# The last layer of the first block works on 258, then 256, of its 272 columns

## The chip, the cores and the metric

The kernel runs on one core of one Trainium2 chip. Its time is the device time of one execution in microseconds (us). Three executions of the kernel before took 2561.17, 2563.9 and 2571.58 us; the median is 2563.9 us.

## What is computed

The reference chains two blocks. The first block puts 16 meta tokens ahead of 256 text tokens, T = 272 in all, and runs two layers over them. The second block runs on the 256 text tokens alone. One layer of the first block, cut to what matters here:

```python
def first_block(...):
    h = jnp.concatenate([meta, x], axis=1)              # 16 + 256 tokens
    for l in range(DEPTH):                              # DEPTH = 2
        u = _rms_norm(h, norm_mix_pre[l])
        (a_q, ..., d_v, gate_logits) = jnp.split(u @ w_in[l], offsets, axis=-1)
        # four mixers: attention over all tokens, chunked recurrence in both directions, ...
        branches = jnp.stack([o_a, o_b, o_c, o_d], axis=2)
        gates = jax.nn.sigmoid(gate_logits.reshape(bsz, T, N_BRANCH, D_MODEL))
        merged = jnp.sum(jnp.einsum('btnw,nwd->btnd', branches, w_branch[l]) * gates, axis=2)
        h = h + _rms_norm(merged @ w_out[l], norm_mix_post[l])
        f = _conv_ffn(_rms_norm(h, norm_ffn_pre[l]), ...)
        h = h + _rms_norm(f, norm_ffn_post[l])
    return h[:, N_META:]

def _conv_ffn(h, w_up, conv_w, conv_b, w_down):
    u = h @ w_up
    up = jnp.pad(u, ((0, 0), (1, 1), (0, 0)))
    u = conv_w[0] * up[:, :-2] + conv_w[1] * up[:, 1:-1] + conv_w[2] * up[:, 2:] + conv_b
    gate, val = jnp.split(u, 2, axis=-1)
    return (jax.nn.gelu(gate, approximate=True) * val) @ w_down
```

The mixers of a layer mix tokens with each other, so they need all 272. Behind them only the convolution of width 3 looks at a neighbour. What leaves the last layer (l = 1) is columns 16 to 271; these need column 15 of the convolution's input, and no column before that. Each of the many matrices is [1024 x 1024], [1024 x 5632] or [2816 x 1024] in float32.

## The kernel before

Activations lie with channels on the 128 partitions and tokens along the free dimension: a tile of 1024 channels is KD = 8 slices of [128, 272]. The weights pass through the core once, cut into 644 slabs of [128, 1024] (512 KB; some 384 KB), in the fixed order of `stream()`. SyncE (SP) loads them into a ring of six buffers, the next load waiting until TensorE (PE) has used the slab six back.

Most products are made in split precision. A slab is cut into a high half `ring_hi` (a rounding copy on ScalarE (ACT), L804, or for some of the projections on VectorE (DVE), L1375) and a low half `ring_lo` (slab minus high half: on VectorE, L1380, or on GpSimd (POOL), L1974). `low_by` gives every slab n of the feed-forward with n % 4 = 3 to GpSimd, the others to VectorE. The halves are made LEAD = 3 slabs ahead of use. The activations have halves `x_hi`, `x_lo` or `hid_hi`, `hid_lo` as well. For each of a slab's 8 pieces of [128 x 128], `split_mm` issues three matmuls: high by high (L347), high weight by low activation (L348), low weight by high activation (L349). So a slab is 24 matmuls, and each streams all columns of the activation. A few products go unsplit, from the raw float32 slab: the branches (L670), the `conv_in` projections (L337) and the sums of squares for the norms (L376, a product with a matrix of ones). For each of these the trace has two matmul records.

The order of the work is written out by hand, one program per engine, the same for both layers. Within a layer behind its projections and mixers:

- `gate(l, j, x)`: 32 gate slabs (4 branches x times 8 channel groups j). Eight of them (j = 0 and 1) stand among the mixers as filler; 24 stand in `merge`.
- `merge(l)`: for each j the four gate slabs (from j = 2) and two branch slabs. VectorE multiplies gate by branch and adds the four up (L1758 to L1765).
- `ffn(l)`: 8 slabs `out`; the norm behind them (sums of squares on TensorE, square root on ScalarE, reciprocal on VectorE, L1402, scaling, then the addition to `h` on GpSimd, L2143); the norm ahead of the feed-forward; 44 slabs `up`, with ScalarE (L1210), VectorE (two steps of L1368 a slab, the convolution taps) and GpSimd (`hidden`, L2107 and L2109, the halves of the hidden activation) behind them; 8 times three slabs `down`; the last norm and the addition to `h` (L2157).

Among these VectorE and GpSimd also work through the `ada` weights of the second block (the load on GpSimd, L1986, the reduction on VectorE, L1397): 144 tiles of 512 KB in all, each put in at a fixed place of the order.

All of this works on `[:, :]` or `0:T`, 272 columns, in both layers. The second block behind it (`swiglu`, slabs `gu` and `down2`, and others) works on 256 columns with the same helpers. The place where the two meet is `sublayer_input(0)`, which reads `h[:, k, S0:T]`, S0 = 16.

Of the kernel before, what the change touches and what calls it, by code (L numbers as in the profile page):

```python
# [166 lines left out]
def build(nc, d, out):  # L167
# [4 lines left out]
    with ctx:  # L172
# [133 lines left out]
        ADA = {"lat": 3, "head": 2, "gla": 3, "mla": 2, "merge": 3}  # L306
        ada_order = [(l, t) for l in range(DEPTH) for t in range(ADA_TILES)]
# [3 lines left out]
        def tensor_program(pe, c):  # L311
# [19 lines left out]
            def project_raw(name, x, cols, by, ready=None):  # L331
                i, _ = begin(name)
                b = claim(slab_bank(name), *by)
                for k in range(KD):
                    if ready:
                        pe.wait_ge(*at(*ready[k]))
                    m = pe.matmul(b[:, 0:cols], ring[:, i, k * P:(k + 1) * P], x[:, k, 0:cols], start=k == 0, stop=k == KD - 1)  # L337
# [14 lines left out]
            def project(name, cols, by, ready=()):  # L352
                split_mm(name, claim(slab_bank(name), *by), x_hi, x_lo, 0, KD, cols, True, True, ready)
# [13 lines left out]
            def project_down(name, j, part, cols, *ready):  # L367
                k0, nk = DOWN[part]
                split_mm(name, bank[slab_bank(name)], hid_hi, hid_lo, k0, nk, cols, part == 0, part == len(DOWN) - 1, *ready)

            def norm(b, name, squares, ready, by, n=T):
# [38 lines left out]
            def gate(l, j, x):  # L410
                project(gate_of(l, j, x), T, (act_, "gate", l, j, x))
# [137 lines left out]
            def mixers(l):  # L549
# [4 lines left out]
                project(("lat", l, 0), T, (act_, "glat", l), [(dve_, "u_lo", l, k) for k in range(KD)])  # L554
                for k in range(3):
                    project(("lat", l, 1 + k), T, (act_, "clat", l, k))
                project(("bq", l, 0), T, (act_, "q", B[0]))
# [1855 lines left out]
```

## Time and profile before

| | |
|---|---|
| median of three runs | 2563.9 us (2561.17 to 2571.58) |
| the profiled execution | 2563.2 us |
| its span, first to last instruction | 2561.4 us |
| mean granted TensorE clock | 0.944 |
| PE busy, share of the span | 2362.2 us, 92% |
| DVE, ACT, POOL busy | 57%, 42%, 32% |
| the chain that ended last | PE 78%, DVE 9%, POOL 4%, DMA 3%, ACT 3% |
| read from HBM | 425.48 MB, 167 GB/s over the span |

Matmuls are pipelined: a record of one lasts some 290 ns, but the next starts some 120 ns after it. What a matmul costs in a dense stretch is the distance from start to start, not the length of its record. "PE busy" counts the time in which at least one is under way.

The second layer's part that is spoken of here runs from 1108.0 us (first branch slab) to 1514.4 us (first slab of the second block) of the span; its eight early gate slabs stand between 936 and 1082 us.

### The profile page before, as it was taken

Reading aid. Unit: us, or ns where it says so; the run is one execution under the profiler, and the core shown is the slowest. Engines: PE = TensorE matmul, PEld = TensorE weight load, DVE = VectorE, ACT = ScalarE, POOL = GpSimd, SP = SyncE. Lnnn points to the kernel's source line nnn. Section 1 sums busy time; section 2 is a strip of 40 time slices with the busy share of each in tenths; the row PEclk is TensorE's granted clock in tenths of the full one; section 3 lists DMA queues with packets and bytes.
Section 4 is the critical chain, followed back from the end, with each engine's and each line's share of the span. In section 5 each row is a group of like instructions: output and inputs, shape, how many; then the busy total and the mean of one; then the engine's idle time right before and its main releaser. Section 6 shows DMA issues by size and latency. Waiting matters only on the chain.

```text
span 2561.4 us, 41098 instructions
## 1 busy us (share of the span) xinstructions
PE 2362.2 (92%) x16612; PEld 2165.6 (85%) x16612; DVE 1452.2 (57%) x2443; ACT 1064.1 (42%) x1930; POOL 812.4 (32%) x769
## 2 busy tenths in 40 slices
PE   6899889989998988999899989999899999988998
PEld 5677659879987777679889979987899999878998
DVE  4665556568857665375488654449544444435443
ACT  4444232255545443222355444432444444445443
POOL 2440002126533431011156434317243243121431
PEclk9998799999999998799999989999899999999999
DMA  6672237536665653257446735554355555533554
GB/s 211 167 183 102 88 117 271 206 122 216 218 210 159 175 167 107 82 189 250 162 148 215 239 129 184 182 156 140 115 184 181 161 184 183 170 120 116 188 179 127
DMA packets 121949, 429.27 MB, mean 168 GB/s; under 512 B 14960, under 2 KB 16928, under 8 KB 121633
## 3 DMA queue, kind: packets, MB, share of 16 engines
q1 hardware_dynamic: 94208, 333.80, 39.8%
q0 software_dynamic: 27408, 91.77, 12.2%
q8 instruction: 133, 2.18, 0.3%
q10 hardware_dynamic: 144, 1.07, 0.1%
q14 instruction: 56, 0.45, 0.1%
HBM read 425.48 MB, written 1.10 MB: 167 GB/s over the span
## 4 chain that ended last, share of the span: by engine, by line
PE 78%; DVE 9%; POOL 4%; DMA 3%; ACT 3%; issue 2%; DVEq 0%; ACTq 0%; POOLq 0%
PE bank L347 20%; PE bank L349 20%; PE bank L348 20%; PE bank L670 5%; DMA ada_ring<-in_ada 3%; PE bank L337 3%; PE bank L376 2%; DVE std L1402 2%; POOL ring_lo L1974 2%; PE bank L407 1%; DVE s_sb L1407 1%; PE bank L498 1%; POOL bias_sb L1996 1%; PE bank L540 1%; PE bank L541 1%
## 5 line engine op out<-in xcount | busy, mean ns | idle before, releaser
L347 PE MATMUL bank<-x_hi,ring_hi 128*128 128x272 f32 (+1 forms) x3552 | 1050.9, 296 | 67.7 <-DVE x_lo L1368 21.2
L349 PE MATMUL bank<-x_hi,ring_lo 128*128 128x272 f32 (+1 forms) x3552 | 1032.0, 291 | 0.0
L348 PE MATMUL bank<-x_lo,ring_hi 128*128 128x272 f32 (+1 forms) x3552 | 1031.4, 290 | 0.0
L1380 DVE TENSOR_TENSOR ring_lo<-ring,ring_hi 128x1024 fp32r<-128x1024 f32 (+1 forms) x437 | 591.0, 1353 | 618.9 <-ACT ring_hi L804 618.9
L347 PEld LDWEIGHTS bank<-x_hi,ring_hi 128*128 128x128 f32 x3552 | 688.6, 194 | 94.1 <-DVE x_lo L1368 18.9
L804 ACT ACTIVATE ring_hi<-ring 128x1024 fp32r<-128x1024 f32 (+1 forms) x551 | 570.7, 1036 | 378.7 <-PE bank L349 276.2
L348 PEld LDWEIGHTS bank<-x_lo,ring_hi 128*128 128x128 f32 x3552 | 689.1, 194 | 0.8
L349 PEld LDWEIGHTS bank<-x_hi,ring_lo 128*128 128x128 f32 x3552 | 689.5, 194 | 0.0
L1974 POOL TENSOR_TENSOR ring_lo<-ring,ring_hi 128x1024 fp32r<-128x1024 f32 (+1 forms) x155 | 373.1, 2408 | 827.5 <-ACT ring_hi L804 506.8
L349 PE MATMUL bank<-hid_hi,ring_lo 128*128 128x256 f32 (+1 forms) x1056 | 300.4, 284 | 0.0
L347 PE MATMUL bank<-hid_hi,ring_hi 128*128 128x256 f32 (+1 forms) x1056 | 299.3, 283 | 0.0
L348 PE MATMUL bank<-hid_lo,ring_hi 128*128 128x256 f32 (+1 forms) x1056 | 298.7, 283 | 0.0
L2107 POOL CAST hid_hi<-cv_sb 128x256 fp32r<-128x256 f32 (+1 forms) x132 | 97.8, 741 | 375.8 <-DVE cv_sb L1845 274.9
L1397 DVE CUSTOM_DVE_ANT_0 ada_ring<-ada_ring,cond 128x1024 f32<-128x1024 f32 x144 | 172.5, 1218 | 60.4 <-DMA ada_ring<-in_ada 60.2
L347 PEld LDWEIGHTS bank<-hid_hi,ring_hi 128*128 128x128 f32 x1056 | 199.3, 189 | 0.0
L348 PEld LDWEIGHTS bank<-hid_lo,ring_hi 128*128 128x128 f32 x1056 | 198.9, 188 | 0.0
L349 PEld LDWEIGHTS bank<-hid_hi,ring_lo 128*128 128x128 f32 x1056 | 198.6, 188 | 0.0
L1986 POOL DMA_DIRECT2D ada_ring<-in_ada x144 | 78.9, 549 | 155.4 <-DVE mod L1397 152.6
L670 PE MATMUL bank<-br,ring 128*128 128x272 f32 x512 | 124.2, 403 | 1.9 <-DVE br L1368 1.9
L670 PEld LDWEIGHTS bank<-br,ring 128*128 128x128 f32 x512 | 99.3, 196 | 23.8 <-DVE br L1368 3.4
L376 PE MATMUL bank<-sq,cst 128*128 128x272 f32 (+1 forms) x284 | 83.8, 448 | 27.5 <-ACT sq L873 13.5
L1368 DVE SCALAR_TENSOR_TENSOR cv_sb<-bank,prm,cv_sb 128x271 f32<-128x271 f32 x176 | 87.6, 498 | 29.7 <-ACT cv_sb L1210 25.4
(275 smaller groups left out, 2312.0 us busy)
## 6 DMA issues: line engine op xcount, KB each, us to landing
ring<-in_w_gu SPq DMA_DIRECT2D x192, 512.0 KB, 3.5
ada_ring<-in_ada POOLq DMA_DIRECT2D x144, 512.0 KB, 5.1
ring<-in_w_in SPq DMA_DIRECT2D x136, 512.0 KB, 4.0
ring<-in_ffn_up SPq DMA_DIRECT2D x104, 512.0 KB, 3.5
ring<-in_w_down SPq DMA_DIRECT2D x64, 512.0 KB, 3.5
ring<-in_w_branch SPq DMA_DIRECT2D x32, 512.0 KB, 3.5
ring<-in_ffn_down SPq DMA_DIRECT2D x32, 512.0 KB, 3.9
ring<-in_w_down SPq DMA_DIRECT2D x32, 384.0 KB, 3.4
```

Of the source, the lines that this page charges most:

```text
L347: pe.matmul(b[:, 0:cols], ring_hi[:, i_hi, c0], x1, start=first and k == 0, stop=False)
L348: pe.matmul(b[:, 0:cols], ring_hi[:, i_hi, c0], x2, start=False, stop=False)
L349: m = pe.matmul(b[:, 0:cols], ring_lo[:, i, c0], x1, start=False, stop=last and k == nk - 1)
L376: m = pe.matmul(ps[:, 0:n], ones, sq[:, k, 0:n], start=i == 0, stop=i == len(squares) - 1)
L670: m = pe.matmul(b[:, 0:T], ring[:, i, (4 * x + k) * P:(4 * x + k + 1) * P], br[:, 4 * (2 * s + x) + k, :], start=k == 0, stop=k == 3)
L804: act.activation(ring_hi[:, n % HIGH, 0:cols], ring[:, i, 0:cols], ACT.Copy).then_inc(*sig(act_, "hi", n))
L1368: return dve.scalar_tensor_tensor(out=out_, in0=a, scalar=s, in1=b, op0=op0, op1=op1).then_inc(*sig(dve_, *name))
L1380: dve.tensor_tensor(ring_lo[:, i, 0:cols], ring[:, i, 0:cols], ring_hi[:, n % HIGH, 0:cols].bitcast(f32), ALU.subtract).then_inc(split(n)[ ...
L1397: dve.tensor_tensor_reduce(out=tile, in0=tile, in1=cond[:, :], scale=1.0, scalar=0.0, op0=ALU.mult, op1=ALU.add, accum_out=mod[:, l * ADA_ ...
L1974: pool.tensor_tensor(ring_lo[:, i, 0:cols], ring[:, i, 0:cols], ring_hi[:, n % HIGH, 0:cols].bitcast(f32), ALU.subtract).then_inc(split(n) ...
L1986: pool.dma_start(ada_ring[:, t % ADA_RING, :], d["ada"][l * ADA_TILES + k]).then_inc(sems[f"ada_loaded{t % ADA_RING}"], 16)
L2107: pool.tensor_copy(hid_hi[:, j, 0:n], at_j).then_inc(*sig(pool_, "hid_hi", *name))
```

## The change

Two slices are defined. `kept(l)` is columns 14 to 271 (258 of them) in the last layer and all 272 in the first; `fed(l)` is columns 16 to 271 (256) in the last layer, all 272 in the first. The helpers take a slice in place of a count of columns. In the last layer

- the gates, branches, merge, `out`, the two norms behind it, the addition of L2143, `up` and the convolution work on `kept`, 258 columns from column 14;
- the GELU, the product of the two halves, the hidden activation's halves, `down`, its norm and the addition of L2157 work on `fed`, 256 columns from column 16.

The first layer, all projections and mixers of the second layer, and the second block keep their sizes. The number and the order of the instructions is the same on each of the five engines, and so are all waits, loads, slabs and buffers; only the lengths along the free dimension and their starts differ. The diff, cut to its core (the other lines of it make the same replacement of `cols`, `n`, `T` or `:` by a slice):

```diff
+        ALL, TEXT = slice(0, T), slice(0, N2)
+
+        def kept(l):
+
+            return slice(N_META - 2 if l == DEPTH - 1 else 0, T)
+
+        def fed(l):
+
+            return slice(N_META if l == DEPTH - 1 else 0, T)
...
-            def split_mm(name, b, hi, lo, k0, nk, cols, first, last, ready=()):
+            def split_mm(name, b, hi, lo, k0, nk, cs, first, last, ready=()):
...
-                    x1, x2 = hi[:, k0 + k, 0:cols], lo[:, k0 + k, 0:cols]
-                    pe.matmul(b[:, 0:cols], ring_hi[:, i_hi, c0], x1, start=first and k == 0, stop=False)
-                    pe.matmul(b[:, 0:cols], ring_hi[:, i_hi, c0], x2, start=False, stop=False)
-                    m = pe.matmul(b[:, 0:cols], ring_lo[:, i, c0], x1, start=False, stop=last and k == nk - 1)
+                    x1, x2 = hi[:, k0 + k, cs], lo[:, k0 + k, cs]
+                    pe.matmul(b[:, cs], ring_hi[:, i_hi, c0], x1, start=first and k == 0, stop=False)
+                    pe.matmul(b[:, cs], ring_hi[:, i_hi, c0], x2, start=False, stop=False)
+                    m = pe.matmul(b[:, cs], ring_lo[:, i, c0], x1, start=False, stop=last and k == nk - 1)
...
-                    m = pe.matmul(ps[:, 0:n], ones, sq[:, k, 0:n], start=i == 0, stop=i == len(squares) - 1)
+                    m = pe.matmul(ps[:, cs], ones, sq[:, k, cs], start=i == 0, stop=i == len(squares) - 1)
...
-                project(gate_of(l, j, x), T, (act_, "gate", l, j, x))
+                project(gate_of(l, j, x), kept(l), (act_, "gate", l, j, x))
...
-                                m = pe.matmul(b[:, 0:T], ring[:, i, (4 * x + k) * P:(4 * x + k + 1) * P], br[:, 4 * (2 * s + x) + k, :],
+                                m = pe.matmul(b[:, kept(l)], ring[:, i, (4 * x + k) * P:(4 * x + k + 1) * P], br[:, 4 * (2 * s + x) + k, kept(l)],
...
-                    split_mm(("out", l, j), b, x_hi, x_lo, 0, KD, T, True, True,
+                    split_mm(("out", l, j), b, x_hi, x_lo, 0, KD, kept(l), True, True,
...
-                norm(NB, ("out", l), range(KD), [("sqo", l, k) for k in range(KD)], (act_, "std", "out", l))
-                norm(NB, ("ffn", l), range(KD), [("sqf", l, k) for k in range(KD)], (act_, "std", "ffn", l))
+                norm(NB, ("out", l), range(KD), [("sqo", l, k) for k in range(KD)], (act_, "std", "out", l), kept(l))
+                norm(NB, ("ffn", l), range(KD), [("sqf", l, k) for k in range(KD)], (act_, "std", "ffn", l), kept(l))
...
-                        split_mm(("up", l, j, gv), b, x_hi, x_lo, 0, KD, T, True, True,
+                        split_mm(("up", l, j, gv), b, x_hi, x_lo, 0, KD, kept(l), True, True,
...
-                        project_down(("down", l, j, part), j, part, T, [(pool_, "hid", l, k0 + k) for k in range(nk)] if j == 0 else ())
-                norm(NB, ("down", l), range(KD), [("sqd", l, k) for k in range(KD)], (act_, "std", "down", l))
+                        project_down(("down", l, j, part), j, part, fed(l), [(pool_, "hid", l, k0 + k) for k in range(nk)] if j == 0 else ())
+                norm(NB, ("down", l), range(KD), [("sqd", l, k) for k in range(KD)], (act_, "std", "down", l), fed(l))
...
-                act.activation(gate_tile(j, x), bank[slab_bank(name)][:, 0:T], ACT.Tanh, scale=0.5,
+                act.activation(gate_tile(j, x)[:, kept(l)], bank[slab_bank(name)][:, kept(l)], ACT.Tanh, scale=0.5,
...
-                        act.activation(cv_sb[:, i, :], bank[slab_bank(("up", l, j, gv))][:, 0:T], ACT.Identity, scale=ap[:, 1:2],
+                        act.activation(cv_sb[:, i, cs], bank[slab_bank(("up", l, j, gv))][:, cs], ACT.Identity, scale=ap[:, 1:2],
...
-                dve.reciprocal(std[:, i, 0:n], std[:, i, 0:n]).then_inc(*sig(dve_, "recip", *name))
+                dve.reciprocal(std[:, i, cs], std[:, i, cs]).then_inc(*sig(dve_, "recip", *name))
...
-                        stt(tmp[:, x, :], gate_tile(j, x), 1.0, bank[merge_bank(j, x)][:, 0:T], ALU.add, ALU.mult, "gated", l, j, x)
+                        stt(tmp[:, x, cs], gate_tile(j, x)[:, cs], 1.0, bank[merge_bank(j, x)][:, cs], ALU.add, ALU.mult, "gated", l, j, x)
...
-                        stt(t[:, 1:T], b[:, 0:T - 1], w[:, 0:1], t[:, 1:T], ALU.mult, ALU.add, "cv2", l, j, gv)
+                        stt(t[:, cs.start + 1:T], b[:, cs.start:T - 1], w[:, 0:1], t[:, cs.start + 1:T], ALU.mult, ALU.add, "cv2", l, j, gv)
                         dve.wait_ge(*at(dve_, "cv2", l, j, gv))
-                        stt(t[:, 0:T - 1], b[:, 1:T], w[:, 2:3], t[:, 0:T - 1], ALU.mult, ALU.add, "cv3", l, j, gv)
-                    g, v = cv_sb[:, 2 * (j % 2), :], cv_sb[:, 2 * (j % 2) + 1, :]
+                        stt(t[:, cs.start:T - 1], b[:, cs.start + 1:T], w[:, 2:3], t[:, cs.start:T - 1], ALU.mult, ALU.add, "cv3", l, j, gv)
+                    g, v = cv_sb[:, 2 * (j % 2), fs], cv_sb[:, 2 * (j % 2) + 1, fs]
...
-                pool.tensor_copy(hid_hi[:, j, 0:n], at_j).then_inc(*sig(pool_, "hid_hi", *name))
+            def hidden(at_j, cs, j, *name):
+                pool.tensor_copy(hid_hi[:, j, cs], at_j[:, cs]).then_inc(*sig(pool_, "hid_hi", *name))
...
-                    pool.tensor_tensor(h[:, k, :], h[:, k, :], u[:, k, :], ALU.add).then_inc(*sig(pool_, "h1", l, k))
+                    pool.tensor_tensor(h[:, k, cs], h[:, k, cs], u[:, k, cs], ALU.add).then_inc(*sig(pool_, "h1", l, k))
...
-                    hidden(cv_sb[:, 2 * (j % 2), :], T, j, "hid", l, j)
+                    hidden(cv_sb[:, 2 * (j % 2), :], fs, j, "hid", l, j)
...
-                    pool.tensor_tensor(h[:, k, :], h[:, k, :], y[:, k, :], ALU.add).then_inc(*sig(pool_, "h2", l, k))
+                    pool.tensor_tensor(h[:, k, fs], h[:, k, fs], y[:, k, fs], ALU.add).then_inc(*sig(pool_, "h2", l, k))
```

## Rows read from the trace of the kernel before

**Rows 1.** The page's busy time: engine, us (share of the span), instructions.
```profile
PE 2362.2 (92%) x16612; PEld 2165.6 (85%) x16612; DVE 1452.2 (57%) x2443; ACT 1064.1 (42%) x1930; POOL 812.4 (32%) x769
```

**Rows 2.** Windows: length, then PE, PEld, DVE, ACT, POOL busy us, clock, DMA share, GB/s.
```profile
996.50:1108.00 111.50, 93.44 (x400) 61.12 (x398) 60.90 (x125) 32.01 (x89) 10.61 (x17) 0.79 0.28 94
1117.60:1246.70 129.10, 124.13 (x801) 114.98 (x800) 82.12 (x134) 33.88 (x53) 27.80 (x28) 1.00 0.70 245
1292.80:1428.70 135.90, 135.78 (x1057) 134.98 (x1058) 121.04 (x173) 77.15 (x116) 77.76 (x63) 0.99 0.63 204
1514.40:1642.00 127.60, 127.52 (x1054) 126.81 (x1055) 60.16 (x68) 56.84 (x74) 50.84 (x53) 0.98 0.54 175
```

**Rows 3.** Timeline of PE: start us, us; starts of slabs `up`, `gu`, `down`, `down2`.
```profile
1340.77 0.29 PE L347 MATMUL bank<-x_hi,ring_hi 128*128 128x272 f32 x1
1352.88 0.29 PE L347 MATMUL bank<-x_hi,ring_hi 128*128 128x272 f32 x1
1523.04 0.28 PE L347 MATMUL bank<-x_hi,ring_hi 128*128 128x256 f32 x1
1534.40 0.28 PE L347 MATMUL bank<-x_hi,ring_hi 128*128 128x256 f32 x1
1436.92 0.29 PE L347 MATMUL bank<-hid_hi,ring_hi 128*128 128x272 f32 x1
1445.20 0.29 PE L347 MATMUL bank<-hid_hi,ring_hi 128*128 128x272 f32 x1
1650.15 0.28 PE L347 MATMUL bank<-hid_hi,ring_hi 128*128 128x256 f32 x1
1657.99 0.28 PE L347 MATMUL bank<-hid_hi,ring_hi 128*128 128x256 f32 x1
```

**Rows 4.** The chain in order of time: unsplit products, 272 and 256 columns.
```profile
1156.67 7.33 PE bank L670 x32
1726.97 13.17 PE bank L337 x61
```

**Rows 5.** The chain between `out` and `up`, in order of time.
```profile
1273.70 3.68 PE bank L376 x16
1280.40 6.46 POOL h L2143 x7
1289.36 1.86 DVE std L1402
```

**Rows 6.** Groups by shape, whole span: busy us, mean ns, idle before, releaser.
```profile
L1402 DVE RECIPROCAL std<-std 128x272 f32<-128x272 f32 x28 | 51.6, 1844 | 25.5 <-ACT std L817 25.5
L1402 DVE RECIPROCAL std<-std 128x256 f32<-128x256 f32 x7 | 12.3, 1753 | 21.4 <-ACT std L817 21.4
L2109 POOL TENSOR_TENSOR hid_lo<-cv_sb,hid_hi 128x256 fp32r<-128x256 f32 x88 | 66.0, 750 | 7.0
L2109 POOL TENSOR_TENSOR hid_lo<-cv_sb,hid_hi 128x272 fp32r<-128x272 f32 x44 | 34.2, 777 | 3.5
L1368 DVE SCALAR_TENSOR_TENSOR u<-h,small,std 128x256 f32<-128x256 f32 x48 | 22.1, 481 | 0.2
L1368 DVE SCALAR_TENSOR_TENSOR u<-h,prm,std 128x272 f32<-128x272 f32 x16 | 7.8, 497 | 0.1
L1368 DVE SCALAR_TENSOR_TENSOR cv_sb<-bank,prm,cv_sb 128x271 f32<-128x271 f32 x176 | 87.6, 498 | 29.7 <-ACT cv_sb L1210 25.4
```

**Rows 7.** Timeline of DVE and POOL in `up` and `down`, in brackets idle before.
```profile
1336.48 3.82 DVE L1380 TENSOR_TENSOR ring_lo<-ring,ring_hi 128x1024 fp32r<-128x1024 f32 x1
1348.59 1.25 DVE L1380 TENSOR_TENSOR ring_lo<-ring,ring_hi 128x1024 fp32r<-128x1024 f32 x1
1349.29 2.82 POOL L1974 TENSOR_TENSOR ring_lo<-ring,ring_hi 128x1024 fp32r<-128x1024 f32 x1
1350.66 1.03 DVE L1368 SCALAR_TENSOR_TENSOR cv_sb<-bank,prm,cv_sb 128x271 f32<-128x271 f32 x2 [0.82 <-ACT cv_sb L1210]
1433.77 2.80 POOL L1974 TENSOR_TENSOR ring_lo<-ring,ring_hi 128x1024 fp32r<-128x1024 f32 x1
```

More of the change, by code:

```diff
@@ L553, in mixers @@
                     bias_lines()
-                project(("lat", l, 0), T, (act_, "glat", l), [(dve_, "u_lo", l, k) for k in range(KD)])
+                project(("lat", l, 0), ALL, (act_, "glat", l), [(dve_, "u_lo", l, k) for k in range(KD)])
                 for k in range(3):
-                    project(("lat", l, 1 + k), T, (act_, "clat", l, k))
-                project(("bq", l, 0), T, (act_, "q", B[0]))
+                    project(("lat", l, 1 + k), ALL, (act_, "clat", l, k))
+                project(("bq", l, 0), ALL, (act_, "q", B[0]))
                 pe.wait_ge(*at(act_, "kpe", l))
@@ L697, in swiglu @@
                         b = claim(slab_bank(("gu", i, j, gv)), *((act_, "silu", i, j) if gv == 0 else (dve_, "hid2", i, j)))
-                        split_mm(("gu", i, j, gv), b, x_hi, x_lo, 0, KD, N2, True, True,
+                        split_mm(("gu", i, j, gv), b, x_hi, x_lo, 0, KD, TEXT, True, True,
                                  [(dve_, "xs_lo", s, k) for k in range(KD)] if j + gv == 0 else ())
@@ L702, in swiglu @@
                     for part, (k0, nk) in enumerate(DOWN):
-                        project_down(("down2", i, j, part), j, part, N2, [(pool_, "hid2", i, k0 + k) for k in range(nk)] if j == 0 else ())
+                        project_down(("down2", i, j, part), j, part, TEXT, [(pool_, "hid2", i, k0 + k) for k in range(nk)] if j == 0 else ())
             def mix_out(layer):
@@ L766, in tensor_program @@
             swiglu(2)
-            norm(NB, ("in2", 4), range(KD), [("sqx", 4, k) for k in range(KD)], (act_, "std", "in2", 4), N2)
+            norm(NB, ("in2", 4), range(KD), [("sqx", 4, k) for k in range(KD)], (act_, "std", "in2", 4), TEXT)
             for i in range(4):
@@ L777, in tensor_program @@
             swiglu(3)
-            norm(NB, ("in2", 6), range(KD), [("sqx", 6, k) for k in range(KD)], (act_, "std", "in2", 6), N2)
+            norm(NB, ("in2", 6), range(KD), [("sqx", 6, k) for k in range(KD)], (act_, "std", "in2", 6), TEXT)
             assert count[0] == len(STREAM)
@@ L812, in halves, with root @@
                             high(n)
-            def root(b, i, name, dim, n, *reader):
+            def root(b, i, name, dim, cs, *reader):
                 act.wait_ge(*at(pe_, "norm", *name))
                 before(("std", i), dve_, *reader)
-                act.activation(std[:, i, 0:n], bank[b][:, 0:n], ACT.Sqrt, scale=1.0 / dim, bias=eps_ap).then_inc(*sig(act_, "std", *name))
+                act.activation(std[:, i, cs], bank[b][:, cs], ACT.Sqrt, scale=1.0 / dim, bias=eps_ap).then_inc(*sig(act_, "std", *name))
             def gate(l, j, x):
@@ L1178, in ffn @@
             def ffn(l):
+                cs, fs = kept(l), fed(l)
                 halves(("out", l, 0))
@@ L1182, in ffn @@
                     act.wait_ge(*at(dve_, "gated", l, k, "y"))
-                    act.activation(x_hi[:, k, :], y[:, k, :], ACT.Copy).then_inc(*sig(act_, "y_hi", l, k))
+                    act.activation(x_hi[:, k, cs], y[:, k, cs], ACT.Copy).then_inc(*sig(act_, "y_hi", l, k))
                 for j in range(KD):
@@ L1231, in sublayer_input @@
                 use_tables(ACT.Sqrt)
-                root(NB, 0, ("in2", s), D_MODEL, N2, *(("ux", s, KD - 1) if s < 6 else ("out", KD - 1)))
+                root(NB, 0, ("in2", s), D_MODEL, TEXT, *(("ux", s, KD - 1) if s < 6 else ("out", KD - 1)))
                 if s == 6:
@@ L1769, in ffn @@
             def ffn(l):
+                cs, fs = kept(l), fed(l)
                 low_halves("out", l, 0)
@@ L2163, in swiglu @@
                     pool.wait_ge(*at(dve_, "hid2", i, j))
-                    hidden(cv_sb[:, j % 2, 0:N2], N2, j, "hid2", i, j)
+                    hidden(cv_sb[:, j % 2, :], TEXT, j, "hid2", i, j)
                 for j in range(KD):
```

167 lines of the change are left out of this document (84 added, 83 removed).

## The prediction

> **What bounds the kernel now.** I read the page's busy time first: TensorE has a matmul under way in 92% of the span [rows 1]. Busy time overcounts here, since matmuls overlap, so next I read windows by stage, to see whether it is TensorE's own pace that bounds the stages the change touches. The reader is to see in the merge window that 124.1 of 129.1 us are busy, in `up` 135.8 of 135.9 us, both at a granted clock of 1.00 or 0.99 [rows 2]. The 5.0 us missing in the first are one wait at its end, for `x_hi`. So these stages are bound by TensorE's start-to-start distance. In the mixers it is otherwise: 93.4 of 111.5 us busy at a clock of 0.79 [rows 2], since attention and recurrence wait on VectorE and ScalarE.
>
> Third, the timeline gives the distance itself. Four `up` slabs are 96 matmuls of 272 columns from 1340.77 to 1352.88: 12.11/96 = 126.1 ns each. Four `gu` slabs, the same 96 matmuls on 256 columns, take 11.36 us: 118.3 ns. One group of `down` (three slabs, 66 matmuls) takes 8.28 us at 272 and 7.84 us at 256, 0.44 us less [rows 3]. Unsplit products take 7.33/32 = 229.1 ns a record at 272 and 13.17/61 = 215.9 ns at 256 [rows 4]. So the kernel itself holds the comparison that the change needs: 16 columns fewer are worth 7.8 ns a split matmul and 13.2 ns a record of an unsplit one.
>
> **The change part by part.** Nothing is added, removed or moved on any engine; the loads are the same 512 KB slabs. Only lengths and starts differ, so no queue is passed and no wait is new. For 258 columns I interpolate between the two rows: 14/16 of 7.8 is 6.8 ns, 14/16 of 13.2 is 11.6 ns.
>
> - Gates in the merge: 24 slabs x 24 matmuls = 576, by 6.8 ns: 3.9 us.
> - Gates among the mixers: 8 x 24 = 192, up to 1.3 us. They are filler in a stage where TensorE is idle 16% of the time; a wait behind them can take it back. I take half, 0.65 us, and keep 0 and 1.3 as ends.
> - Branches: 16 slabs x 16 records = 256, by 11.6 ns: 3.0 us.
> - `out`: 192 matmuls, 1.3 us.
> - `up`: 44 x 24 = 1056 matmuls, 7.2 us, if nothing else steps in front (below).
> - `down`: 8 groups by 0.44 us, straight from the rows: 3.5 us.
> - The chains in which TensorE waits. Between `out` and `up` the chain goes through 16 records of L376, the reciprocal twice, seven additions on GpSimd and a few short links [rows 5]. A record saves 11.6 ns: 0.19 us. A reciprocal of 272 takes 1844 ns and one of 256 takes 1753: 0.08 us each at 258, twice [rows 6]. GpSimd's two-input operation takes 777 ns at 272 and 750 at 256, 1.7 ns a column [rows 6], so 7 x 24 ns = 0.17 us; were all its 923 ns by the column, it would be 0.33. A VectorE operation goes from 497 to 481 ns over 16 columns [rows 6], 14 ns at 258; some twenty such links here (VectorE feeds `x_lo` slice by slice at the start of `up`) give 0.35 us. Together 0.9 us. The chain between `down` and the second block has the same parts once, at 256 columns, and is unchanged behind them: 16 x 13.2 + 91 + 7 x 27 ns, 0.5 us. Behind the merge five short links give 0.1 us. Sum 1.5 us; ends 1.2 and 1.8.
>
> **What is late next in `up`.** A faster TensorE asks for its halves sooner, so I looked at who has least room. VectorE is busy 121.0 of 135.9 us in `up` [rows 2], against 60.2 of 127.6 in `gu`: the convolution and the `ada` reductions are its extra load. Its work repeats every 8 slabs (24.2 us), with three idle times, of 0.82 us [rows 7], 0.85 and 0.37. So VectorE needs 22.2 us; 16 operations of L1368 and four products at 14 to 16 ns less make it 21.9. TensorE's 8 slabs will take 8 x 2.863 = 22.9 us. It fits, by 1.0 us.
>
> The narrower spot is the low half that GpSimd makes of every fourth slab. The one that begins at 1349.29 and lasts 2.82 us ends at 1352.11 [rows 7], and TensorE starts that slab at 1352.88 [rows 3]: 0.77 us of room. Its chain goes back through the hidden halves to VectorE, which has been behind since a 3.82 us operation at 1336.48 [rows 7], and is free of TensorE for six slabs. Six slabs get 0.98 us shorter; the chain loses about 0.2 us (four pairs of L1368, two products, one activation, one subtraction). The room comes out at 0.77 - 0.98 + 0.2 = 0.0 us. So the gain in `up` just fits, with nothing over: I take off 0.8 us for small waits, some 0.15 us in each of the five and a half periods. That makes `up` 6.4 us. The first slab of `down` that GpSimd cuts has the same kind of chain: its low half ends at 1433.77 + 2.80 = 1436.57 [rows 7], its first matmul starts at 1436.92 [rows 3], 0.35 us of room. TensorE comes 0.44 us sooner, the chain 0.1 us, and it fits too.
>
> The 3.82 us are a collision: the operation takes 1.25 us when it begins 0.70 us ahead of GpSimd's [rows 7], and sits out most of GpSimd's when it comes at the wrong moment. A shift of a few tenths of a us could turn a free one into a colliding one, the second rival below. The operations of L1368, which read PSUM and one SBUF tile, last 498 ns in either case [rows 6]. The Trainium skill ("GPSIMD Engine Reference", Key points) says that GpSimd shares its SBUF interfaces with VectorE and contends with instructions that have two SBUF inputs; both rows agree with it, and it speaks for that rival.
>
> **Sum.** 3.9 + 0.65 + 3.0 + 1.3 + 6.4 + 3.5 + 1.5 = 20.3 us off the profiled execution's own 2563.2 us (its span is 1.8 us less): 2542.9 us. The median of the runs shown is 0.7 us above the profiled one, so 2543 to 2543.6; I say 2543.
>
> The unknown is the 258 columns from column 14, a size and a start that no matmul here has. If what does not scale with columns stays that of the 256-column matmul, plain scaling at 2.4 GHz, the full level, gives 107.5 + 11.7 = 119.2 ns; with that of the 272-column one, 107.5 + 12.8 = 120.3 ns. These bracket my 119.3, and the latter takes 1.0 x 1824 = 1.8 us from the gain. The Trainium skill ("TensorE: Matmul & The Clock Gate", Back-to-back issue gap) gives N/2.4 plus a constant; an estimate by that page is 5.8 ns for 14 columns, and the sum would be some 18.5 us.
>
> **Rivals.**
>
> *The 14 columns buy nothing in split products.* If the streaming goes by blocks of 16 columns, columns 14 to 271 touch the same 17 blocks as 0 to 271, and the distance stays 126.1 ns. For it: 272 and 256 are both whole blocks, so the rows cannot exclude it. Against it: the 7.8 ns between them is close to 16 single columns (6.7 ns). `down`, which starts on a block's edge, keeps its gain, and so do branches and chains: 3.5 + 3.0 + 1.5 = 8.0 us, 2555 us. The Trainium skill's sustained figures in the same section (about 81 ns at N = 128 and 131 at N = 512) make a column worth only 0.13 ns, an estimate of 1.8 ns for the 14, where the rows show 0.49 ns a column; by that the split products would give some 3 us in all, close to this rival.
>
> *VectorE takes over in `up`.* If the operation that now runs free 0.70 us ahead of GpSimd's collides as well, VectorE needs 21.9 + 2.6 = 24.5 us for 8 slabs, against 24.2 us now. Then `up` gets 5.5 x 0.3 = 1.6 us longer in place of 6.4 shorter, and the time is 2563.2 - (20.3 - 8.0) = 2551 us. For it: my working of the two queues leaves them 0.6 us apart there instead of 0.70. Against it: that is a small move, and the collision that exists may just as well dissolve.
>
> *The start at column 14 is dear (slower).* If a start off the 16-column grid, in SBUF or in PSUM, costs one block more than the 17, the split matmul goes to 126.1 + 7.8 = 133.9 ns and the unsplit record to 229.1 + 13.2 ns. That is 1824 x 7.8 = 14.2 us and 256 x 13.2 = 3.4 us more, less 5.0 for `down` and the chains: 12.6 us slower, 2576 us. It decides from 130.5 ns on, with branches unchanged at that point (8.0/1824 = 4.4 ns). For it: no TensorE access in the trace starts off that grid. Against it: VectorE's L1368 on 271 columns starts at column 1 and takes 498 ns, the aligned one on 272 takes 497 [rows 6].
>
> That the change does not do what it says I exclude: the order of instructions is the same and the lengths are those stated.
>
> **How the numbers follow.** Forecast 0.78; nothing for 14 columns 0.08; VectorE bound 0.09; dear start 0.05. The forecast's own spread is about 3 us each way: 1.8 us of the unknown pace, 0.65 of the mixers' gates, and stretches of half clock that fall differently in each run. The range of 2537 to 2552 holds the forecast and most of the second rival. A measurement of this kernel tells 0.5% (12.8 us) from no change; faster means under 2551. That is the forecast and about half of the VectorE case, 0.81; within is the other half and the first rival, 0.14; slower 0.05.
>
> **What would show it.** Right: `up` slabs 2.86 us apart, `down` groups 7.84, branch records 217.5 ns, the room of GpSimd's low half near zero with waits of TensorE on L1974 of a few tenths of a us in `up`. Wrong: split matmuls at 126 ns or more in gates, `out` and `up` (first or third rival), or slabs in `up` well over 2.86 us apart behind VectorE busy over 97% (second). It would also be wrong if the mixers' stage or the second block changed its length, which I hold fixed but for half of eight gates.

## The result and the profile after

| | before | after |
|---|---|---|
| median | 2564.3 us (2561.2 to 2572.3, 7 runs) | 2551.7 us (2541.7 to 2553.4, 7 runs) |
| profiled execution | 2563.2 us | 2553.2 us |
| its span, mean granted clock | 2561.4 us, 0.944 | 2551.4 us, 0.944 |

The ratio after/before is 0.9929 with an interval of 0.9916 to 0.9943, that is 18.2 us less (14.6 to 21.5). 2543 us had been forecast, with a range of 2537 to 2552: the sign was right, and the median lies at the slow edge of the range, 0.3 us inside it. The 20.3 us forecast as a difference lie inside the interval. But the medians of the table are only 12.6 us apart, and the two profiled executions 10.0 us. Whole times leave the size of the gain open; most of this section is about what settles it.

The page's busy time, against [rows 1]:

```profile
PE 2347.3 (92%) x16612; PEld 2149.0 (84%) x16612; DVE 1457.9 (57%) x2443; ACT 1061.8 (42%) x1930; POOL 800.2 (31%) x769
```

The counts are those of before. The windows of the merge, of `up`, and of `down` with its chain, all of after, and then the merge of before; columns are length, then PE, PEld, DVE, ACT, POOL busy us with counts, granted clock, DMA share, GB/s:

```profile
1115.40:1247.90 132.50, 127.02 (x832) 118.80 (x833) 86.19 (x141) 34.66 (x54) 28.80 (x30) 0.98 0.72 250
1292.00:1423.10 131.10, 130.24 (x1057) 129.24 (x1058) 122.86 (x173) 76.27 (x116) 76.72 (x63) 0.98 0.63 212
1423.10:1504.75 81.65, 72.94 (x563) 69.27 (x561) 46.02 (x56) 36.09 (x57) 26.18 (x23) 0.94 0.60 195
```

```profile
1108.03:1246.72 138.69, 133.70 (x832) 122.66 (x833) 86.34 (x141) 34.94 (x54) 28.86 (x30) 0.98 0.69 239
```

The second answers to the third of [rows 2]: `up` fell from 135.8 to 131.1 us, and VectorE is busy 1.8 us longer there, not shorter. The merge is counted here from its first branch slab, 9.6 us ahead of the start in [rows 2]; both end at the first slab of `out`, so both hold the wait for `x_hi`.

Stages are compared by the first matmul of each stage's first slab, in us:

| stage | before | before, second profile | after, three profiles | forecast | first pair |
|---|---|---|---|---|---|
| first layer | 754.5 | 760.6 | 758.3, 754.8, 757.7 | none | +3.8 |
| second layer up to its first gate | 162.6 | 162.9 | 165.6, 162.4, 162.3 | none | +2.9 |
| mixers with eight gates | 171.9 | 171.7 | 172.1, 172.0, 173.1 | -0.65 | +0.3 |
| merge | 138.7 | 138.7 | 132.5, 132.7, 131.5 | -7.0 | -6.2 |
| `out` and its chain | 46.1 | 46.1 | 44.1, 43.6, 43.8 | -2.2 | -2.0 |
| `up` | 135.8 | 135.9 | 131.1, 130.8, 131.0 | -6.4 | -4.7 |
| `down` and its chain | 85.8 | 85.8 | 81.7, 81.6, 81.7 | -4.0 | -4.1 |

The four stages that the change shortens lost 17.1 us in the first pair, and 17.7 on the mean of the three profiles of after; forecast were 19.6. Outside them the first pair differs by +7.1 us, in work that is the same in both kernels. The second profile of before, kernel unchanged, is 6.1 us longer than the first in the first layer alone. Over the twelve profiles of this document, in all of which the first layer has the same instructions, it takes 751.0 to 762.4 us, and the second layer's projections 161.9 to 165.6. So 7.1 us are within the scatter between executions, and they lie mostly where TensorE waits on others (the first layer, and the second's projections and mixers); `merge`, `out`, `up` and `down` of the two profiles of before agree within 0.1 us. For a change of this size the stage lengths are the sharper instrument.

The distances, as starts of slabs (us) in TensorE's timeline; twice four slabs of `up`, then one group of `down`, against [rows 3]:

```profile
1306.34 0.28 PE L357 MATMUL bank<-x_hi,ring_hi 128*128 128x258 f32 x1
1317.83 0.28 PE L357 MATMUL bank<-x_hi,ring_hi 128*128 128x258 f32 x1
1405.59 0.28 PE L357 MATMUL bank<-x_hi,ring_hi 128*128 128x258 f32 x1
1417.01 0.28 PE L357 MATMUL bank<-x_hi,ring_hi 128*128 128x258 f32 x1
1433.99 0.28 PE L357 MATMUL bank<-hid_hi,ring_hi 128*128 128x256 f32 x1
1441.81 0.28 PE L357 MATMUL bank<-hid_hi,ring_hi 128*128 128x256 f32 x1
```

11.49/96 = 119.7 ns in the first pair and 11.42/96 = 119.0 ns in the second, and 7.82 us for the group. The unsplit products, in the chain in order of time:

```profile
1162.55 6.96 PE bank L680 x32
```

6.96/32 = 217.5 ns, the interpolated value to the digit ([rows 4] has 7.33 at 272 columns).

What `up` did not give shows as small waits behind GpSimd's low half. The timeline of POOL, then that of PE, at one of them:

```profile
1346.31 0.57 POOL L1999 DMA_DIRECT2D ada_ring<-in_ada  x1
1346.90 2.82 POOL L1987 TENSOR_TENSOR ring_lo<-ring,ring_hi 128x1024 fp32r<-128x1024 f32 x1
```

```profile
1349.56 0.28 PE L359 MATMUL bank<-x_hi,ring_lo 128*128 128x258 f32 x1
1349.86 0.36 PE L357 MATMUL bank<-x_hi,ring_hi 128*128 128x258 f32 x1
```

The low half ends at 1349.72 and the slab starts 0.14 us later, 0.30 us behind the last matmul instead of 0.12. In before there were 0.77 us of room here ([rows 7] and [rows 3]). One such wait comes every 8 slabs, five in all. Counted over two slabs (the late one and the one before it) against the pace of their neighbours, they cost 0.24, 0.25, 0.95, 0.23 and 0.37 us. The third is larger, since GpSimd's queue issued the load in front of the low half late; again POOL, then PE (in brackets the idle time before):

```profile
1370.63 0.57 POOL L1999 DMA_DIRECT2D ada_ring<-in_ada  x1 [1.05 <-issue]
1371.22 2.39 POOL L1987 TENSOR_TENSOR ring_lo<-ring,ring_hi 128x1024 fp32r<-128x1024 f32 x1
```

```profile
1373.75 0.36 PE L357 MATMUL bank<-x_hi,ring_hi 128*128 128x258 f32 x1 [0.72 <-POOL ring_lo L1987]
```

Together 2.0 us of waits in `up`, and 2.2 us in each of the two later profiles of after, with the large one, 0.9 us, at the same slab. It is no accident of one execution: the late issue stands at this slab in the trace of before too. POOL and PE there:

```profile
1373.99 0.57 POOL L1986 DMA_DIRECT2D ada_ring<-in_ada  x1 [1.01 <-issue]
1374.58 2.41 POOL L1974 TENSOR_TENSOR ring_lo<-ring,ring_hi 128x1024 fp32r<-128x1024 f32 x1
```

```profile
1377.14 0.36 PE L347 MATMUL bank<-x_hi,ring_hi 128*128 128x272 f32 x1
```

That low half ends at 1376.99 and its slab starts 0.15 us later: the room was used up in before already, at a cost of 0.1 us. So what TensorE gained on GpSimd up to this slab (0.98 - 0.2 us by the prediction's working) came back as a wait, 0.95 us where there had been 0.1.

In the merge there is a wait that the forecast did not have. The chain of waits in order of time (start, us, work):

```profile
1132.64 5.88 DMA ada_ring<-in_ada
1138.55 1.23 DVE ada_ring L1408
1139.78 1.15 DVE ring_lo L1391
1140.93 0.14 issue
1141.07 0.36 PE bank L357
```

VectorE's low half of one gate slab stands behind an `ada` reduction whose tile is still being loaded, and TensorE waits for it. The idle time in the trace is 0.58 us here and 1.13 and 0.21 in the other two profiles of after; from start to start of slabs, against 118.9 ns a matmul, it costs 0.8, 1.4 and 0.5 us. In before VectorE already waited for that same tile, 0.67 us; in after it is 1.37 us. The two rows, from the timelines of before and of after:

```profile
1130.83 1.23 DVE L1397 CUSTOM_DVE_ANT_0 ada_ring<-ada_ring,cond 128x1024 f32<-128x1024 f32 x1 [0.67 <-DMA ada_ring<-in_ada]
```

```profile
1138.55 1.23 DVE L1408 CUSTOM_DVE_ANT_0 ada_ring<-ada_ring,cond 128x1024 f32<-128x1024 f32 x1 [1.37 <-DMA ada_ring<-in_ada]
```

### The profile page after: what moved, and what is told of

The parts are those of the page before. It is cut to its first block, busy times and chain, and to the rows that moved or that the text cites. A ratio compares the mean times of both kernels' runs of the same rounds, so it can differ in the third digit from the quotient of the medians.

```text
span 2551.4 us, 41098 instructions
## 1 busy us (share of the span) xinstructions
PE 2347.3 (92%) x16612; PEld 2149.0 (84%) x16612; DVE 1457.9 (57%) x2443; ACT 1061.8 (42%) x1930; POOL 800.2 (31%) x769
## 4 chain that ended last, share of the span: by engine, by line
PE 76%; DVE 12%; DMA 4%; POOL 4%; ACT 3%; issue 2%; DVEq 0%; ACTq 0%; POOLq 0%
PE bank L357 20%; PE bank L359 20%; PE bank L358 20%; PE bank L680 4%; DMA ada_ring<-in_ada 4%; PE bank L386 3%; DVE s_sb L1379 2%; POOL ring_lo L1987 2%; DVE std L1413 2%; PE bank L417 1%; DVE ring_lo L1391 1%; DVE s_sb L1418 1%; PE bank L347 1%; PE bank L508 1%; PE bank L550 1%
## 5 line engine op out<-in xcount | busy, mean ns | idle before, releaser
L357 PE MATMUL bank<-x_hi,ring_hi 128*128 128x256 f32 (+2 forms) x3552 | 1045.7, 294 | 70.7 <-DVE x_lo L1379 21.2
L358 PE MATMUL bank<-x_lo,ring_hi 128*128 128x256 f32 (+2 forms) x3552 | 1029.1, 290 | 0.0
L359 PE MATMUL bank<-x_hi,ring_lo 128*128 128x256 f32 (+2 forms) x3552 | 1026.1, 289 | 0.0
L680 PE MATMUL bank<-br,ring 128*128 128x272 f32 (+1 forms) x512 | 121.4, 398 | 2.3 <-DVE br L1379 2.3
L680 PEld LDWEIGHTS bank<-br,ring 128*128 128x128 f32 x512 | 99.5, 196 | 21.3 <-DVE br L1379 3.8
L386 PE MATMUL bank<-sq,cst 128*128 128x272 f32 (+2 forms) x284 | 83.6, 449 | 26.9 <-ACT sq L883 13.3
L2122 POOL TENSOR_TENSOR hid_lo<-cv_sb,hid_hi 128x256 fp32r<-128x256 f32 (+1 forms) x132 | 99.4, 753 | 10.6
```

Of the source, the lines that this page charges most:

```text
L357: pe.matmul(b[:, cs], ring_hi[:, i_hi, c0], x1, start=first and k == 0, stop=False)
L358: pe.matmul(b[:, cs], ring_hi[:, i_hi, c0], x2, start=False, stop=False)
L359: m = pe.matmul(b[:, cs], ring_lo[:, i, c0], x1, start=False, stop=last and k == nk - 1)
L386: m = pe.matmul(ps[:, cs], ones, sq[:, k, cs], start=i == 0, stop=i == len(squares) - 1)
L680: m = pe.matmul(b[:, kept(l)], ring[:, i, (4 * x + k) * P:(4 * x + k + 1) * P], br[:, 4 * (2 * s + x) + k, kept(l)], start=k == 0, stop=k ...
L2122: pool.tensor_tensor(hid_lo[:, j, cs], at_j[:, cs], hid_hi[:, j, cs].bitcast(f32), ALU.subtract).then_inc(*sig(pool_, *name))
```

## Experiments

The theory after the result: the pace did what was interpolated, 7.8 ns a split matmul at 256 columns and some 6.7 at 258; some 3 us of it went into the two kinds of wait above, of which 0.8 had been forecast; the rest of the difference between the profiles is scatter. The rivals: streaming in blocks of 16, a price for the start at column 14, and a real loss in the unchanged stages.

**The kernel before, and the kernel after, once more.** No edit. These separate scatter from loss.

> The kernel before, unchanged, for a second profile. In the first pair of profiles the stages that the change touches got 17.1 us shorter, yet the span only 10.0 us: stages with the same instructions got 7.1 us longer (first layer up to the second one's first slab +3.8, its mixers +2.9, the convolution stage +2.2, others less). Theory A: those are differences from run to run, in the stages where TensorE waits and its clock falls; then this profile differs from the first one of before by several us in the first layer and the mixers, and by under 0.3 us in merge, up and down. Rival B: the change lengthens them; then this profile repeats the first one's stages within 1 us.

Measured: 2571.8 us, span 2570.0 at a clock of 0.943, 8.6 us over the first profile of the same kernel. The first layer has +6.1, the last `conv_in` group of the second block +2.4; the stages of the change agree within 0.03 us.

> The changed kernel, unchanged, timed in five rounds, with a second profile. Theory A: merge, out, up and down repeat their lengths (132.5, 44.1, 131.1 and 81.7 us from first slab to the next stage's first slab) within 0.5 us, the unchanged stages scatter by several us, and the ratio is 0.9934 (17 us), between 0.992 and 0.995. Rival B: the first layer and the mixers repeat the longer times of the first profile after, 758.3 and 165.6 us, within 1 us, and the ratio is 0.996.

Measured: ratio 0.9921 (0.9895 to 0.9947), span 2543.6 us. Merge 132.7, `out` 43.6, `up` 130.8, `down` 81.6: the changed stages repeat within 0.5 us, and the unchanged ones come back to within 0.4 us of the first profile of before. A loss there that always comes with the change is excluded.

**One half of the change at a time.** `out`, `up` and `down` keep the fewer columns; gates and branches go back to 272:

```
- project(gate_of(l, j, x), kept(l), ...)
+ project(gate_of(l, j, x), ALL, ...)      # likewise branches, gate activation, merge
```

> The changed kernel with gates, branches and merge of the last layer back on 272 columns; out, up, down and their norms on 258 and 256. Theory: the parts add up; merge back to 138.7 us, the others as in the changed kernel, so -10.9 us against before (ratio 0.9958, 0.9945 to 0.997). Rival: the stalls on GpSimd's low half in up come from the merge's new timing; then up is shorter here than 131.1 us, by 1 us or more.

Measured: ratio 0.9944 (0.9920 to 0.9968), merge 138.7, `up` 131.2, `down` 81.6. The stages are as expected, the ratio just under its expected range. `up` isn't shorter than in after, and its five waits are there, so they don't come from the merge's new timing.

And the other half, with columns 14 to 271 in gates and branches, 272 in everything behind the merge (`kept` and `fed` give ALL; a new `merged` gives the 258 columns to gates, branches and merge):

> Only gates, branches and merge of the last layer on 258 columns; out, norms, up and down on 272 (what stands in columns 0 to 13 of the merged activation is then left from earlier work; it reaches no output). Theory: merge 132.5 us, all behind it as before, -6.2 us against before (ratio 0.9976, 0.996 to 0.999), and no stall of TensorE on ring_lo in up. Rival: gates that stand among the mixers give their 1.3 us as well, -7.5 us.

Measured: ratio 0.9978 (0.9958 to 0.9998), merge 133.6, `out` 45.4, `up` 135.8, `down` 85.8. Each half shortens its own stages and no others, but for 0.7 us of `out`'s chain; -5.1 and -0.7 here, and -2.1, -4.6, -4.1 there, make 16.6 of the 17.1 us. The 0.7 us had not been expected, and the merge is 1.1 us longer than expected. `up` has no new wait, as expected, and the stage of the mixers (171.7) doesn't show the rival's 1.3 us. The two parts hardly act on each other. Here the wait in the merge is at its largest; the timeline of PE:

```profile
1142.61 0.36 PE L361 MATMUL bank<-x_hi,ring_hi 128*128 128x258 f32 x1 [1.74 <-DVE ring_lo L1395]
```

Over all profiles with fewer than 272 columns in the merge's gates and the two `ada` tiles in their place this wait is 0.21, 0.21, 0.32, 0.58, 0.58, 0.81, 1.13 and 1.74 us; in the three with 272 columns it is not there. It hangs on when a load of 512 KB lands (5.88 us above), which is most of why the merge varies from 131.5 to 133.6 us at 258 columns and by 0.02 us at 272. The other part is its start, where TensorE waits for the last of the mixers' results: the first 32 records of the branches take 9.2, 8.9 and 8.5 us in after and 9.1 here. With both taken off, all four merges are 122.5 us.

**Does the start at column 14 cost anything?** The same number of columns, from column 0 instead; the last 14 (or 16) of the sequence are left out in place of the first, so its output leaves out columns that are read. `fed` (256 columns) and the two convolution taps follow in the same way.

```
- return slice(N_META - 2 if l == DEPTH - 1 else 0, T)      # kept
+ return slice(0, T - N_META + 2 if l == DEPTH - 1 else T)
```

> The changed kernel with the same widths, 258 and 256, but from column 0: the last 14 or 16 columns of the last layer are left out instead of the first, so the last text tokens come out stale. Theory: the start costs nothing; pace 118.9 to 119.7 ns a split matmul, 217.5 ns a record of L680, time of the changed kernel within 0.15%. Rival: a start at column 14 costs some ns a matmul; then merge is shorter than 132.5 us by 1 us or more and the ratio is 0.001 or more below that of the changed kernel.

Measured: ratio 0.9928 (0.9904 to 0.9952); merge 131.9, `out` 43.5, `up` 131.1, `down` 81.7. The window of `up`:

```profile
1288.55:1419.61 131.06, 130.31 (x1057) 129.31 (x1057) 122.69 (x173) 76.28 (x116) 76.69 (x63) 0.98 0.63 212
```

This is after's row again, to 0.04 us in length. From column 0 nearly all split matmuls of gates and `up` are 119.7 to 120.0 ns apart, from column 14 they are 118.9 to 119.7, and records of L680 217.5 ns in both. The start at column 14 costs nothing here.

**What does a column cost between 256 and 272?** Gates and `up` of the second layer take start columns 0, 2, ... 14 in turn, for j = 0 to 7, so widths from 272 to 258 stand side by side. The kernel ran once.

```
+ STARTS = (0, 2, 4, 6, 8, 10, 12, 14)
+ def some(l, j): return slice(STARTS[j % 8] if l == DEPTH - 1 else 0, T)
```

> The changed kernel, but TensorE streams 272, 270, 268, 266, 264, 262, 260, 258 columns in the gate slabs and up slabs of j = 0 to 7 (and again from j = 8) of the last layer; the other engines stay on 258. It measures the pace against the width. Theory 1 (a column is a column, 0.42 to 0.49 ns each): 126.1, 125.2, 124.2, ... 119.3, steps of 0.8 to 1.0 ns for two columns. Rival (blocks): the pace stays at 126.1 down to some width and falls at once.

Measured: span 2557.5 us. Starts of pairs of slabs in `up` (48 matmuls each), from the timeline:

```profile
1303.91 0.29 PE L363 MATMUL bank<-x_hi,ring_hi 128*128 128x270 f32 x1
1309.88 0.29 PE L363 MATMUL bank<-x_hi,ring_hi 128*128 128x268 f32 x1
1315.82 0.28 PE L363 MATMUL bank<-x_hi,ring_hi 128*128 128x266 f32 x1
1321.74 0.29 PE L363 MATMUL bank<-x_hi,ring_hi 128*128 128x264 f32 x1
1327.58 0.29 PE L363 MATMUL bank<-x_hi,ring_hi 128*128 128x262 f32 x1
1333.42 0.28 PE L363 MATMUL bank<-x_hi,ring_hi 128*128 128x260 f32 x1
1339.15 0.28 PE L363 MATMUL bank<-x_hi,ring_hi 128*128 128x258 f32 x1
1344.88 0.29 PE L363 MATMUL bank<-x_hi,ring_hi 128*128 128x272 f32 x1
```

The differences, divided by 48: 124.4 ns at 270, 123.8 at 268, 123.3 at 266, 121.7 at 264 and at 262, 119.4 at 260 and at 258. With 126.1 at 272 and 118.3 at 256 [rows 3] it is a stair with steps of 0 to 2.3 ns: neither one block of 16 nor an even slope, so neither expectation held. 262 and 264 cost the same, as do 258 and 260. The slabs from j = 8 on repeat these values within 0.2 ns wherever TensorE doesn't wait. The gates have 122.2 ns at 268 columns, then 123.3, 121.7, 121.7, 119.1 and 118.9 from 266 down to 258. Since one width can have paces 0.8 ns apart (last section), only the larger steps are certain. The rival "14 columns buy nothing" is excluded. Its mixers stage took 178.9 us against 171.7 to 173.7 in the other profiles. The expectation did not have that, and one profile can't say whether it is scatter.

**The small wait in `up`.** GpSimd issues the `ada` load behind its low half instead of in front of it:

```
+ if l == DEPTH - 1 and gv == 0 and j and j % 2 == 0:
+     ada(1)                    # after this slab's low half
- if j % 2:
+ if j % 2 and (l < DEPTH - 1 or j == NJ - 1):
```

> The changed kernel, but in up of the last layer GpSimd issues the ada load behind the low half of the fourth slab and not ahead of it; nothing else moves. Theory: TensorE's stalls in up (0.24 us in each group of 8 slabs, and 0.9 us once, when that load was issued 1 us late) are the room of GpSimd's low half, which grows by the 0.57 us of the issue; up goes from 131.1 to about 129 us, ratio to before 0.001 lower than the changed kernel's. Rival: VectorE is the bound (busy 122.9 of 131.1 us); then up stays at 131 us within 0.5.

Measured: ratio 0.9916 (0.9892 to 0.9940), `up` 128.7 us. The window of `up`; two starts in TensorE's timeline that are 8 slabs apart; GpSimd between them, at the slab that waited in after:

```profile
1281.07:1409.81 128.74, 128.74 (x1057) 128.64 (x1058) 116.95 (x173) 76.21 (x116) 78.73 (x63) 0.98 0.64 213
```

```profile
1306.61 0.28 PE L357 MATMUL bank<-x_hi,ring_hi 128*128 128x258 f32 x1
1329.54 0.28 PE L357 MATMUL bank<-x_hi,ring_hi 128*128 128x258 f32 x1
```

```profile
1311.40 3.39 POOL L1987 TENSOR_TENSOR ring_lo<-ring,ring_hi 128x1024 fp32r<-128x1024 f32 x1
1314.74 0.57 POOL L1999 DMA_DIRECT2D ada_ring<-in_ada  x1
```

22.93/192 = 119.4 ns straight through a period that held a wait before, and TensorE is busy for the whole window. `up` is 2.1 to 2.4 us shorter than in the three profiles of after, about the 2.0 to 2.2 us of waits counted there. Nothing else was moved, so the place of that issue is the cause. How it acts is less simple than the theory had it. The low half ends at 1314.79 and its slab starts at 1315.21, 0.42 us later; but it begins 1.0 us earlier than in after, counted from the slab ahead of it, now nearly together with VectorE's, and takes 3.39 us instead of 2.81, which gives over half of that back. VectorE's long ones got shorter, 3.3 us instead of 3.9, and VectorE is busy 117.0 of 128.7 us. In after it was busy 122.9 of 131.1, but its free low halves stayed free (1.32 us), and the waits behind the first slab are GpSimd's, so it was not the bound.

**The `ada` work out of `up` altogether.** VectorE's reductions and the loads of the second half of `mod` go to the first swiglu of the second block, which has room [rows 2]:

```
- if j % 2:                     # in up
+ if j % 2 and l < DEPTH - 1:
+ if i == 0 and j % 2: ada(1)   # in swiglu; the bias added in two halves
```

> The changed kernel with the 11 ada tiles of up in the last layer worked off in the first swiglu of the second block, where VectorE is busy 59 of 125 us; the modulation's bias is added in two halves, and order and number of the rest stay. Theory: both the room of GpSimd's low half and VectorE's load are relieved by 1.3 us in 4 slabs; up goes to 44 x 2.87 + 2.8 = 128.9 us or less, and the swiglu keeps its 127.9 us; 2 us less than the changed kernel. Rival: the loads of 512 KB and the reductions cost as much there, or push VectorE and GpSimd into collisions; no change in the sum.

Measured: ratio 0.9908 (0.9888 to 0.9928), `up` 128.4 us, VectorE busy 104.7 us there. The windows of `up` and of the swiglu:

```profile
1289.51:1417.90 128.39, 128.39 (x1056) 128.29 (x1057) 104.65 (x153) 76.17 (x116) 60.15 (x53) 0.98 0.55 175
1499.20:1627.00 127.80, 127.60 (x1055) 126.90 (x1056) 77.44 (x88) 56.82 (x74) 74.28 (x62) 0.98 0.63 212
```

Taking another 12 us off VectorE goes with 0.3 us over the kernel before it. Not even that is shown to come from VectorE: split matmuls are 118.9 ns apart in this `up` and 119.4 to 119.5 in the one before, a difference that the last section can't explain and that is worth 0.5 us. The swiglu (127.9 in after) takes the work for nothing.

**Both waits removed.** As above, and the two `ada` tiles at j = 1 of the second layer's merge, the later of which VectorE waits for, also move into the swiglu:

```
- if j < 2:
+ if j < 2 and not (l == DEPTH - 1 and j == 1):
```

> As ada_moved, and the two ada tiles that stand behind the merge's second channel group (j = 1, last layer) go to the first swiglu too. In all four profiles with a merge on 258 columns TensorE stood before the fourth gate slab of the first full group, for 0.4 to 1.9 us, waiting for a low half of VectorE; on 272 columns it did not. Theory: VectorE makes that low half behind ada tiles, one of which waits for its load; with two tiles fewer that slab starts on time, the third gate slab takes 2.87 us in place of 3.2 to 4.8, merge is 131.2 us or less, up 128.4, and the time 3 us below the changed kernel (ratio to before 0.991). Rival: the wait is for the load of the next ada tile whatever stands before it; merge stays at 131.6 to 132.7 us.

Measured: ratio 0.9913 (0.9884 to 0.9943), span 2550.2, merge 131.1, `up` 129.5. The starts of three slabs around the place of the wait:

```profile
1136.57 0.28 PE L357 MATMUL bank<-x_hi,ring_hi 128*128 128x258 f32 x1
1139.42 0.28 PE L357 MATMUL bank<-x_hi,ring_hi 128*128 128x258 f32 x1
1142.27 0.38 PE L680 MATMUL bank<-br,ring 128*128 128x258 f32 x1
```

2.85 us each, no wait, where each of the eight profiles with these tiles in place has one: the cause of the merge's wait is shown. `up` missed its expectation of 128.4: it ran at 119.7 ns, where the two kernels before it had 119.4 and below. The sum of the merge and `up` is 260.6 us, against 263.2 on the mean of after's three profiles and 260.0 with the tiles in the merge left alone, so this version isn't better than the one before it. Its time, expected 3 us below that of the changed kernel, is 2551.4 us against 2551.7 in the same comparison (next run).

> The changed kernel once more, on the same chip as best: ratio to before 0.9925 within 0.002; merge 132.6, out 43.8, up 131.0, down 81.6 us within 0.7; the pace of split matmuls on 258 columns at 118.9, 119.5 or 119.7 ns, changing only where TensorE has waited.

Measured: 2551.7 us median, ratio 0.9921 (0.9895 to 0.9946), merge 131.5, `up` 131.0. The intervals of the three kernels before it (0.9884 to 0.9943 together) overlap after's almost wholly. That they are 2.6 to 3.2 us shorter in the merge and `up` together is shown by the stages, not by their times.

## Why the prediction was right, and where its sizes were off

- **The pace.** 258 columns were interpolated at 119.3 ns with bounds of 119.2 and 120.3. Measured: 118.9 in most of the gates, 118.9 to 119.7 in `up`. The value was good to 0.4 ns, though the line it was drawn on is a stair. At 260 columns the same line gives 120.2, and 119.4 was measured.
- **Branches and `down`.** 217.5 ns and 7.84 us forecast, 217.5 and 7.82 measured; with its chain `down` gave 4.1 us for 4.0.
- **`out` and its chain.** 2.2 forecast, 2.0 to 2.5 measured.
- **`up`.** 6.4 forecast, 4.8 on the mean. The place (GpSimd's low half, every 8 slabs) and the room of zero were right; the term for small waits was mis-sized, 2.0 to 2.2 us and not 0.8. Four waits were some 0.3 us instead of 0.15: the room of 0.77 us was taken whole, though 0.14 us lie between the end of a low half and the start of its slab even when TensorE waits. One was 0.9 us because a DMA issue in front of the low half came 1.05 us late. This one could have been read ahead of time, as the same issue is 1.01 us late in before; the prediction worked out one period, around 1349 us, and took it for all.
- **Merge.** 7.0 forecast, 6.4 on the mean. The room was examined in `up` and `down` but not here. The `ada` tile that VectorE waits for, with 0.67 us in before's timeline, was the nearest thing to a bound, and costs 0.5 to 1.4 us in the three profiles of after. Gates at 118.9 ns instead of 119.3 gave 0.2 us back.
- **Gates among the mixers.** 0.65 was carried as half of 1.3. 171.9 and 171.7 of before stand against 172.1, 172.0 and 173.1: no gain to be seen, and less than 1 us can't be told there.
- **What was held fixed.** It is fixed on the mean, but an execution varies by 6 us in the first layer. The forecast put 3 us on this and the unknown pace together, and a single profile of before was taken as the base. That base was a low one: the medians of before in the later comparisons are 2569 to 2574 us, those of after 2550 to 2552. The difference was forecast better (20.3, against 17.7 in the stages and 14.6 to 21.5 in the times) than the absolute time, 8.7 us off. That 2551.7 falls inside the range is partly luck. The range reached to 2552 to take in the second rival, which did not come; what filled that room was scatter in work that the change doesn't touch, and 0.3 us more would have left it.
- **The chances.** They don't add up to the last digit: 0.78 and half of 0.09 make 0.825 for "faster", and 0.81 was said.
- **Rivals.** The widths exclude the first. The second, VectorE as the bound, does not hold: the operation that ran free still runs free, and moving one GpSimd issue brings the stage to TensorE's pace. The start at column 14 is free, which excludes the third.

## What to carry to other kernels

When a bound engine gets faster by a per cent or two, list every producer's room at the time it is needed, in each stage and not only in the busiest one; rooms under a microsecond are where the gain leaks. A load's issue that stands in a queue ahead of an operation with no room is worth moving behind it. List the rooms for every repetition of a loop, not for one: the one slab of 44 whose room was gone already stood in the trace of before. And compare stages, with the kernel before profiled twice, before a difference outside the change is explained at all.

## What the runs showed that was not expected

- The distance of a split matmul between 256 and 272 columns is a stair, above. The Trainium skill ("TensorE: Matmul & The Clock Gate", Back-to-back issue gap) has N/2.4 plus a constant for the gap of a single matmul, an even slope of 0.42 ns a column; the runs have 7.8 ns over 16 columns, 0.49 ns a column, in uneven steps.
- At 258 columns the pace has three values, 118.9, 119.4 to 119.5 and 119.7 ns. It keeps one over many slabs and changes only where TensorE has waited. It is worth 0.8 us in `up`. Why is open, and no run here tells.
- VectorE's low half takes 1.22 us when free, and up to 3.9 us when it begins 0.3 to 0.4 us ahead of GpSimd's; 0.7 to 0.8 us ahead, it stays free at 1.3 us and GpSimd's takes 2.8 instead of 2.4. At under 0.1 us ahead, in the kernel with the issue moved, it is free as well (1.22) and GpSimd's takes 3.4. In after the order did not flip.
- One stage far from the change has two lengths, 34.3 and 36.7 us: in the second block, from its fifth-last `conv_in` slab to the first slab behind them, in work that no kernel here changes. Both profiles of one kernel, the one before, show one each. The twelve profiles are six of each kind, and the kinds differ in where GpSimd is held up. Four GpSimd products of this stage (`br<-br` of [128 x 256]) are alike; the next one of the same form behind each takes 0.73 us. In the 34.3 kind three of the four take 6.2, 7.8 and 9.7 us, in the 36.7 kind two take 6.2 and 8.9, and TensorE waits 1.4 us once among those last slabs. The last slow one in before, then in after, each with the VectorE operations beside it:

```profile
1770.27 9.70 POOL L2182 TENSOR_TENSOR br<-br 128x256 f32<-128x256 f32 x1 [8.42 <-ACT br L1299]
1767.91 11.57 DVE L1368 SCALAR_TENSOR_TENSOR s_sb<-br,prm,s_sb 128x256 f32<-128x256 f32 x29
1746.48 8.95 POOL L2196 TENSOR_TENSOR br<-br 128x256 f32<-128x256 f32 x1 [8.38 <-ACT br L1310]
1743.76 11.17 DVE L1379 SCALAR_TENSOR_TENSOR s_sb<-br,prm,s_sb 128x256 f32<-128x256 f32 x28
```

  Each ends 0.5 us behind the end of VectorE's unbroken run (1779.48 and 1754.93), and so do the other slow ones of these two profiles: here a GpSimd operation of 0.7 us was held until VectorE's run was over. What decides between the two kinds in an execution is open.
